# Differential attention: the rotary row swap done by small SBUF transfers instead of a product with a permutation matrix

## The reference, cut to what matters

```python
q = rotary(q.reshape(B, L, 2 * H, d), pos, ROPE_THETA, ROT_DIM)   # ROT_DIM = 64 // 4 = 16
k = rotary(k.reshape(B, L, 2 * H, d), pos, ROPE_THETA, ROT_DIM)
# rotary: x1, x2 = first 8 and next 8 of the 16 rotated dims
rot = concatenate([x1 * cos - x2 * sin, x2 * cos + x1 * sin])      # the other 48 dims pass through
# diff_attention, for each block of 128 queries:
a = softmax(q1 k1^T * scale + mask) - lam * softmax(q2 k2^T * scale + mask)
o = a @ v
```

## Time and profile before

| | |
|---|---|
| median of 3 runs | 3183.58 us (3179.44 to 3187.36) |
| profiled execution, its own time | 3182.52 us |
| its span in the trace | 3180.7 us |
| mean granted TensorE clock (1 is full) | 0.973 |
| PE busy / DVE / ACT / POOL | 95% / 64% / 40% / 38% of the span |
| differential attention with its first two projections | about 1813 to 2033 us of the span |

### The profile page before, as it was taken

How to read it: one execution, slowest core, us unless ns; L and a number is a source line. 1 busy time by engine, 2 the same in 40 slices (tenths; PEclk the granted TensorE clock), 3 DMA queues, 4 the chain that set the end, 5 groups by cost and what they waited for, 6 DMA issues and landing times.

```text
span 3180.7 us, 47766 instructions
## 1 busy us (share of the span) xinstructions
PE 3011.1 (95%) x17737; PEld 2623.4 (82%) x17737; DVE 2027.4 (64%) x3225; ACT 1264.7 (40%) x2171; POOL 1202.9 (38%) x576
## 2 busy tenths in 40 slices
PE   5998899998989999999999999899999999999998
PEld 2766578998888888888887788699999975899976
DVE  4576614999978778788886355466651465466622
ACT  2347433445963333333333334432222446432221
POOL 1520233675225444455553312044434530244443
PEclk8998999999999999999999999699999999999999
DMA  5630123555579999999996211032223220122321
GB/s 215 231 132 1 48 92 89 169 170 179 221 251 345 345 334 343 334 350 349 344 341 227 66 47 47 7 93 91 87 86 97 84 80 1 41 93 92 92 92 68
DMA packets 181093, 507.07 MB, mean 159 GB/s; under 512 B 15840, under 2 KB 73184, under 8 KB 176736
## 3 DMA queue, kind: packets, MB, share of 16 engines
q1 hardware_dynamic: 72000, 262.18, 25.1%
q0 software_dynamic: 36864, 134.23, 11.3%
q10 hardware_dynamic: 72096, 108.93, 10.2%
HBM read 465.43 MB, written 39.85 MB: 159 GB/s over the span
## 4 chain that ended last, share of the span: by engine, by line
PE 84%; DVE 6%; ACT 6%; issue 2%; DMA 1%; ACTq 0%; DVEq 0%
PE ps L1274 23%; PE ps L1225 17%; PE ps L1162 15%; PE ps L1522 8%; PE ps L897 6%; ACT arena L1938 2%; PE ps L1339 2%; PE ps L947 1%; PE ps L1405 1%; ACT arena L1954 1%; PE ps L1669 1%; DVE arena L2344 1%; PE ps L1412 1%; PE ps L1292 1%; PE ps L1448 1%
## 5 line engine op out<-in xcount | busy, mean ns | idle before, releaser
L2292 POOL TENSOR_TENSOR w_lo<-ring,w_hi 128x1024 fp32r<-128x1024 f32 x312 | 789.5, 2533 | 1547.0 <-ACT w_hi L793 1546.6
L793 ACT ACTIVATE w_hi<-ring 128x1024 fp32r<-128x1024 f32 x500 | 525.4, 1055 | 780.5 <-PE ps L1225 264.0
L1225 PE MATMUL ps<-w_hi,arena_r 128*128 128x512 f32 x1536 | 427.3, 397 | 5.2 <-DVE arena_r L2730 5.2
L1162 PE MATMUL ps<-h_hi,w_hi 128*128 128x384 f32 x1024 | 354.9, 347 | 4.6 <-issue 4.6
L1274 PE MATMUL ps<-h_hi,w_hi 128*128 128x264 f32 (+2 forms) x1536 | 348.2, 299 | 4.8 <-DVE arena L2827 4.8
L1225 PEld LDWEIGHTS ps<-w_hi,arena_r 128*128 128x128 f32 x1536 | 289.2, 189 | 73.3 <-DVE arena_r L2730 6.0
L1162 PE MATMUL ps<-h_lo,w_hi 128*128 128x384 f32 x1024 | 348.3, 340 | 0.0
L1274 PE MATMUL ps<-h_lo,w_hi 128*128 128x264 f32 (+2 forms) x1536 | 347.1, 298 | 0.0
L1274 PE MATMUL ps<-h_hi,w_lo 128*128 128x264 f32 (+2 forms) x1536 | 346.4, 298 | 0.0
L1162 PE MATMUL ps<-h_hi,w_lo 128*128 128x384 f32 x1024 | 345.8, 338 | 0.0
L2719 DVE TENSOR_TENSOR w_lo<-ring,w_hi 128x1024 fp32r<-128x1024 f32 x188 | 228.5, 1222 | 134.1 <-ACT w_hi L793 132.7
(11 more groups left out here) (343 smaller groups left out, 5487.7 us busy)
## 6 DMA issues: line engine op xcount, KB each, us to landing
ring<-weight_stream SPq DMA_DIRECT2D x500, 512.0 KB
gates<-arena ACTq DMA_DIRECT2D x12, 2048.0 KB, 7.2
arena<-gates ACTq DMA_DIRECT2D x32, 768.0 KB, 14.4
arena<-w_modulation ACTq DMA_DIRECT2D x16, 1024.0 KB, 5.2
early_acts<-arena ACTq DMA_DIRECT2D x64, 192.0 KB
arena<-early_acts ACTq DMA_DIRECT2D x32, 384.0 KB, 7.4
arena<-w_modulation ACTq DMA_DIRECT2D x4, 2048.0 KB, 24.3
x<-x_t ACTq DMA_DIRECT2D x1, 2048.0 KB, 11.8
```

The source lines that it names most:

```text
L793: act.activation(w_hi[:, s, :], ring[:, s, :], ACT.Copy).then_inc(hi_ready, 1)
L1162: last = pe.matmul(ps[:, bank, 0:ND], w, v, start=c == 0 and p == 0, stop=c == DC - 1 and p == 2)
L1225: last = pe.matmul(ps[:, Y_BANKS[b][half], :], a[u], w[v][:, half * BANK:(half + 1) * BANK], start=first and p == 0, stop=final and p == 2)
L2292: pool.tensor_tensor(w_lo[:, s, :], ring[:, s, :], w_hi[:, s, :], ALU.subtract)\
```

## The change

The product with the swap matrix is gone from this stage (the later latent attention keeps it). After `raw_copy(t)` ACT waits for its own copy to finish and issues four transfers inside SBUF, of 8 partitions by 528 columns each, that put the 8 + 8 rotated rows of both maps into `tmp_d` in swapped order. `tmp_d` is zeroed once by DVE before the stage, and the sine table has the minus sign in the low rows. DVE waits for the four transfers (`swapped_in`) and multiplies `tmp_d` by sin in place, now from SBUF. `project(t)` waits only for the copy of tile t-1 (`raw_taken`). The odd units have no PE work ahead any more. Semaphores of lambda are merged into `meta_pe` and `meta_act`, with the counts moved by one.

```diff
+ROT = DIFF_DIM // 4
+SWAPS = 4
@@ PE
-                    pe.wait_ge(rope_step, 3 * (t - 1) + 2)
+                    pe.wait_ge(raw_taken, t)
                 tile2("qk_diff", TURN["qk_diff"] + t // RING, t % RING, qk_tile(t)[1])
-
-            def rotate(t):
-
-                pe.wait_ge(raw_taken, t + 1)
-                rot(raw_d[:, t % 2, :], qk_tile(t)[1]).then_inc(rot_ready, 1)
...
             project(0)
             project(1)
-            rotate(0)
-            rotate(1)
...
                 if b % 2 == 0:
                     project(t)
-                else:
-                    rotate(t)
@@ ACT, raw_copy
                 act.activation(split(raw_d[:, t % 2, :]), pair(qk_tile(t)[1]), ACT.Copy).then_inc(raw_taken, 1)
+                act.wait_ge(raw_taken, t + 1)
+                for m in range(2):
+                    for low in range(2):
+                        to, src = DIFF_DIM * m + ROT // 2 * low, DIFF_DIM * m + ROT // 2 * (1 - low)
+                        act.dma_start(tmp_d[to:to + ROT // 2, t % 2, :], raw_d[src:src + ROT // 2, t % 2, :])\
+                            .then_inc(swapped_in[t % 2], 16)
                 split_next(act, "qk_diff", t // RING, t % RING)
@@ DVE
+            dve.memset(tmp_d, 0.0)
             dve.tensor_tensor(lam_p, vec[:, o:o + 2], vec[:, o + 2:o + 4], ALU.mult).then_inc(lam_step, 1)
...
-                dve.wait_ge(rot_ready, t + 1)
-                dve.tensor_tensor(split(tmp_d[:, t % 2, :]), pair(banks), split(tab("sin")), ALU.mult)\
-                    .then_inc(rope_step, 1)
+                dve.wait_ge(swapped_in[t % 2], 16 * SWAPS * (t // 2 + 1))
+                dve.tensor_tensor(tmp_d[:, t % 2, :], tmp_d[:, t % 2, :], tab("sin"), ALU.mult).then_inc(rope_step, 1)
@@ host table
+                if kind == 0:
+                    sin[lo] = -sin[lo]
```

More of the change, by code:

```diff
@@ L62 @@
 ROPE_STEPS = 2 + PER_ROPE
-DIFF_META_STEPS, DIFF_META_ACTS = 7, 3
+ROT = DIFF_DIM // 4
+SWAPS = 4
+DIFF_META_STEPS, DIFF_META_ACTS = 7, 4
 DIFF_RECS = 3 * DIFF_HEADS * TB
@@ L533, in build @@
         rot_ready = sem("rot_ready")
+        swapped_in = [sem(f"swapped_in{k}") for k in range(2)]
         rope_step = sem("rope_step")
@@ L536, in build @@
         lam_step = sem("lam_step")
-        lam_sum = sem("lam_sum")
-        lam_exp = sem("lam_exp")
         meta_step = sem("meta_step")
@@ L1356, in _ @@
             pe.wait_ge(lam_step, 1)
-            pe.matmul(ps[:, 0, 0:2], ones, lam_p, start=True, stop=True).then_inc(lam_sum, 1)
+            pe.matmul(ps[:, 0, 0:2], ones, lam_p, start=True, stop=True).then_inc(meta_pe, 1)
             project(0)
             project(1)
-            rotate(0)
-            rotate(1)
             def meta_scores():
@@ L1379, in meta_out @@
             def meta_out():
-                pe.wait_ge(meta_act, 2)
+                pe.wait_ge(meta_act, 3)
                 for h in range(8):
@@ L1449, in d_out @@
                 last.then_inc(av_done, 1)
-            pe.wait_ge(lam_exp, 1)
+            pe.wait_ge(meta_act, 1)
             pe.wait_ge(lam_step, 5)
@@ L2074, in _ @@
             value_copies(1)
-            act.wait_ge(lam_sum, 1)
-            act.activation(lam_e, ps[:, 0, 0:2], ACT.Exp).then_inc(lam_exp, 1)
+            act.wait_ge(meta_pe, 1)
+            act.activation(lam_e, ps[:, 0, 0:2], ACT.Exp).then_inc(meta_act, 1)
             raw_copy(0)
@@ L2120, in _ @@
                     d_probs(u)
-            act.wait_ge(meta_pe, 2)
+            act.wait_ge(meta_pe, 3)
             act.activation(amT[0:META, 0:8, :], ps[0:META, 4, 0:P].rearrange("p (a b) -> p a b", b=META), ACT.Copy)\
                 .then_inc(meta_act, 1)
-            act.wait_ge(meta_pe, 3)
+            act.wait_ge(meta_pe, 4)
             act.activation(o_d[:, :, 0:META], ps[:, 5, 0:P].rearrange("p (a b) -> p a b", b=META), ACT.Copy)\
                 .then_inc(meta_act, 1)
-            act.wait_ge(meta_act, 3)
+            act.wait_ge(meta_act, 4)
             def high_head(c):
@@ L2821, in rope_parts @@
             def rope_parts(t):
-                dst, banks = qk_tile(t)
+                dst = qk_tile(t)[0]
                 dve.wait_ge(raw_taken, t + 1)
                 dve.tensor_tensor(qk_d[:, dst, :], raw_d[:, t % 2, :], tab("cos"), ALU.mult).then_inc(rope_step, 1)
-                dve.wait_ge(rot_ready, t + 1)
-                dve.tensor_tensor(split(tmp_d[:, t % 2, :]), pair(banks), split(tab("sin")), ALU.mult)\
-                    .then_inc(rope_step, 1)
+                dve.wait_ge(swapped_in[t % 2], 16 * SWAPS * (t // 2 + 1))
+                dve.tensor_tensor(tmp_d[:, t % 2, :], tmp_d[:, t % 2, :], tab("sin"), ALU.mult).then_inc(rope_step, 1)
             def rope_join(t):
@@ L2834, in _ @@
             dve.tensor_copy(mask_rows[0:65, P:P + CHUNK], cst("lowest", CHUNK, 65)).then_inc(lam_step, 1)
-            dve.wait_ge(lam_exp, 1)
+            dve.wait_ge(meta_act, 1)
             dve.scalar_tensor_tensor(neg_lam, lam_e[:, 1:2], LAM_INIT, lam_e[:, 0:1], ALU.subtract, ALU.subtract)\
@@ L2847, in meta_shift @@
             def meta_shift():
-                dve.wait_ge(meta_pe, 1)
+                dve.wait_ge(meta_pe, 2)
                 for m in range(2):
@@ L2859, in meta_probs @@
             def meta_probs():
-                dve.wait_ge(meta_act, 1)
+                dve.wait_ge(meta_act, 2)
                 dve.tensor_reduce(pm_sum[0:META, :], pm[0:META, :, :], AX, ALU.add).then_inc(meta_step, 1)
@@ L3020, in _ @@
             dve.tensor_tensor(kr, kr_raw, tab("cos"), ALU.mult).then_inc(rope_step, 1)
-            dve.wait_ge(rot_ready, QK_TILES + 1)
+            dve.wait_ge(rot_ready, 1)
             dve.wait_ge(rope_step, 3 * QK_TILES + 1)
@@ L3045, in query_rope @@
                 raw, tmp = raw_m[:, t, :], tmp_m[:, t % 2, :]
-                dve.wait_ge(rot_ready, QK_TILES + 1 + t + 1)
+                dve.wait_ge(rot_ready, 1 + t + 1)
                 if t >= 2:
```

## The result

The changed kernel takes **3234.48 us**, the median of 4 runs (3229.76 to 3244.62), and the kernel before 3184.03 us beside it (4 runs, 3179.44 to 3187.36): ratio 1.0166, 95% interval 1.0142 to 1.0189. The change makes the kernel 50 us slower. The forecast was 3198 us, 15 slower, with a range of 3181 to 3209.

A forecast was written before the change was run, and what follows sets the result against it. PE, busy 95% of the span, was taken to bound the kernel. Terms summed to +0.6 us at full clock, plus 15 for clock falls: +15.6 on 3182.5 gave 3198 us, range 3181 to 3209.

The forecast's parts named there:

- The start, -7.5 us: Start of the stage: projection 2 begins 5.3 us sooner and runs 2.5 us faster at full clock, less 0.3.
- The last term: Start of the stage: the first scores wait for tile 1's joined sine and cosine products, losing 0.3 us.
- The four transfers: ACT's queue behind the raw copy: four issues at 0.33 us each, bounds 0.15 and 0.56, delay what follows.
- x: Delay of everything of ACT behind the raw copy, caused by the four issues: 1.65 us.
- Units b = 1 and b = 3: Odd units of heads 1 to 6: PE waits for ACT's late keep (+6.6 us) and late exponentials (+2.0).
- Head 0 has no output copy: nothing: Head 0 at b = 3: ACT's exponentials are not delayed, so no time is lost there.
- The clock, +15 us: Attention loop: the b = 1 stall halves PE's clock once in each of heads 1 to 6, 2.5 us each.
- DVE: DVE's sine product, with two SBUF inputs, waits for POOL; mostly hidden by projections, +0.3 us in head 6.
- Theory C: Stated with the experiments: late landing of the transfers holds DVE up, and PE behind it; no size given.
- rival 4: Landings above 5 us delay DVE's maxima; each further us costs one at the start; no separate chance given.
- Rival 3: ACT's issues cost 0.5 us each and the clock falls more: 3208 to 3213 us; chance 0.06 for dearer than 3209.

The follow-up runs named there:

- The kernel with the filled stalls: Changed kernel plus rotation products nobody reads, three at b = 1 and two at b = 3, where the rotations stood; issues still on ACT: 3203.34 us.
- the useless product: One rotation product nobody reads added ahead of each unit b = 3, on the changed kernel with its transfers issued by SyncE: 3170.98 us.
- the SyncE kernel: Changed kernel with the same four transfers per tile issued from SyncE's queue, between its weight refills, instead of ACT's: 3170.66 us, ratio 0.9965.
- the kernel with two issues: Changed kernel with two of its four transfers per tile, the second map's rows not swapped: 3201.25 us, ratio 1.0057.
- the kernel with one: Changed kernel with one of its four transfers per tile, moving only 8 rows of the first map: 3183.59 us, ratio 1.0001.

## Why the prediction was too low

**The start, -7.5 us: right in kind, 1.4 too good.** Projection 2 needs ACT's copy alone and runs at full clock, as said. The last term was mis-sized, again by the issues: I let the first scores lose 0.3 us, and they wait 1.5 us for the join. The transfers are issued over 2.6 us rather than 1.5, and the first sine product was held under POOL's for 2.79 us. Measured: -6.1. With the issues on SyncE, or behind the split, the first scores don't wait for the join and the start is 7.4 us shorter than before the change.

**The four transfers: the step that failed.** "One takes 0.33 us at least"; I took 0.33, with 0.56 as the upper bound, by issues from and to HBM. Measured 0.632, outside the bound. No row of before had a transfer with both ends in SBUF, and a longer list of rows of the wrong kind didn't make the bound better. One row that the prediction left out stood above it already, a load from HBM with a median of 0.72 us:

```profile
L1964 ACTq DMA_DIRECT2D arena<-gates x32: 525/723/9625, 930.9 to 1637.3; - x32
```

The lateness of ACT is the split at 1931.51 less the copy's end at 1928.76, plus the 0.10 that it used to be ahead: x = 2.85 us instead of 1.65.

**Units b = 1 and b = 3: right at b = 1, in part at b = 3; the size follows x.** With the slack that the prediction had read, b = 1 costs x - 0.56 = 2.29 and b = 3 x - 1.32 = 1.53 us a head. The kernel with the filled stalls shows 5.7 - 3.5 = 2.2 and 4.8 - 3.3 = 1.5. For six heads 13.7 + 9.2, less 0.8 for head 0, and 0.3 at the end: **+22.4** where the prediction had +8.1. That the rotation at b = 3 gives nothing is shown by the useless product, and that the scores there can wait for the exponentials by the waits of the SyncE kernel. But the prediction left out that at b = 3 PE needs `keep` before that. `keep` of b = 2 ended at 1897.62, and the transposes began behind it at 1899.15:

```profile
1899.15 0.36 PEld L1412 LDWEIGHTS ps<-const,arena 128*128 128x128 f32 x2
```

So the delay by that path is x - 1.43 = 1.42 us, and with the missing 0.77 us of the rotation it gives the stall of 2.19 that the changed kernel shows. The two paths are 0.1 us apart, so this cost the sum little in heads 1 to 6. In head 0 it did count: "Head 0 has no output copy: nothing" was wrong. From the scores of its b = 0 to the next head's it takes 25.7 us where it took 21.8; the one fall of the clock in it can explain at most 3.4 of the 3.9, so head 0 lost at least 0.5 by waiting instead of gaining 0.8.

**The clock, +15 us: right mechanism, wrong number of falls.** It fell twelve times, not six: behind the stalls at b = 3 too, which were 2.2 us and not 1.2. That their length made the difference fits the kernel with two issues (three falls behind seven such stalls of about 1 us). The loop and tail lost 54.8 us; without the 22.4 of waiting 32.4 remain (31.1 at most with what head 0 showed), 2.7 for each fall, close to the 2.5 that came from the earlier trace rows. Where a fall costs was not as predicted: not "most of the next projection" but its first 0.6 to 3.3 us and the products ahead of it; the projections behind the stalls took 6.2 to 7.4 us instead of 5.9. The kernel with two issues gives 2.1 a fall (24.0 more in its loop, less 0.84 x 6 + 0.08 x 6 - 0.8 + 0.3 = 5.0, over nine falls). The time at half clock is the better measure. A mean of 0.81 over 217.3 us is 83 us of it, a mean of 0.88 over 186.1 is 45: the loss is 0.4 us for each of these us in both kernels. Filling the stalls gave 31 us back, so the clock is shown as a cause of its own, the larger one. Its number of falls can't be worked out from the stalls' length alone: behind stalls of 1.1 us it sometimes fell and mostly held.

**DVE: right.** Its sine product takes 2.76 us beside POOL's work; the old one, with an input in PSUM, took 0.70. In the Trainium skill, page "SBUF — State Buffer", section "Who interferes with whom", an operation with two SBUF inputs is blocked by a GpSimd operation that reads SBUF and started first. The trace agrees: POOL's 2.34 us began at 1932.65, the sine product at 1932.79, and it ended 0.56 us behind POOL's. In the loop it is covered. Theory C, rival 4 of the prediction, falls: transfers of 16 partitions landed 2.0 us after their issue (median), the sine product began 2.0 us after the last issue of 8 partitions (1930.78 to 1932.79), and the SyncE kernel keeps all the transfers.

**In sum** -6.1 + 22.4 + 32.4 = +48.7, and 4.2 between the executions in the rest of the program, make the 52.9 of the spans. The 32.4 is what was left over, so the sum proves nothing by itself; its check are the 31 us of the filled stalls. Rival 3, dearer issues, was what happened, but its price of 0.5 us was too low as well: it gave 3208 to 3213.

**Left open:** why two ends in SBUF and 8 partitions make an issue longer; why the start alone brings 3 to 4 us in the median and 6 in the trace.

## What to carry to other kernels

A DMA isn't free for the engine that issues it: count its issues as work in that engine's order, and put them on a queue with nothing urgent behind them. The same change is 50 us slower with the issues on ACT and **some 12 us faster, 3171 us, with them on SyncE**, the best version here. Price an unknown issue by one of its own kind (source, target, partitions, its neighbours), and where there is none let the upper bound be twice the nearest row (here 0.33 was known and 0.63 came). Before taking work off TensorE, look at what it will wait for in its place: a stall among thin products can cost twice, its own length and the clock of the products behind it.

## What the runs showed of the hardware that was not expected

- Issue of one transfer: 0.32 us for 16 partitions from HBM, 0.51 for 8 partitions from HBM; inside SBUF 0.51 for 16 and 128 partitions and 0.54 for 32 as the first one, 0.61 for 16 and 64 right behind another one, and 0.63 for 8 partitions in any place, on ACT and (0.62) on SyncE alike.
- A transfer inside SBUF landed 1.9 us after its issue at the least with 16 partitions and 2.4 us with 128, at the most 3.8.
- Five useless rotation products a head made the program 31 us faster (3234 to 3203 us), by keeping the loop's clock at 0.99 instead of 0.81.
- Stalls of at most 1.8 us in front of thin products were enough to halve the clock nine times in the kernel with two issues, and stalls of at most 1.2 us three times in the kernel with one.
